# Two layers written out, a bank-by-bank end of the down projection, and the next stage's sums and splits made in quarters

## The reference, cut to what matters

```python
for l in range(DEPTH_2):                       # 2 layers
    x = x + 0.5 * swiglu(rms_norm_2(x, ffn1_norm[l]), ffn1_w_gate[l], ffn1_w_up[l], ffn1_w_down[l])
    h = rms_norm_2(x, mix_norm[l])
    z = h @ w_in[l]
    ...                                        # two attentions on z, gates g, "merged"
    x = x + merged @ w_out[l]
    x = x + 0.5 * swiglu(rms_norm_2(x, ffn2_norm[l]), ffn2_w_gate[l], ffn2_w_up[l], ffn2_w_down[l])

def rms_norm_2(x, g):
    return x * lax.rsqrt(jnp.mean(x * x, axis=-1, keepdims=True) + EPS) * g
def swiglu(x, w_gate, w_up, w_down):           # w_gate, w_up: 1024 x 2816, w_down: 2816 x 1024
    return (silu(x @ w_gate) * (x @ w_up)) @ w_down
```

## Time and profile before

| | us |
|---|---|
| runs: median (lowest to highest, 3) | 3258.0 (3250.89 to 3263.54) |
| the profiled execution, its own time | 3250.51 |
| its span | 3248.8 |
| TensorE busy | 2921.2 (90%) |
| VectorE, ScalarE, GpSimd busy | 1820.7, 1488.0, 708.0 |

### The profile page before, as it was taken

One profiled execution on the slowest core, in us unless ns is written; L12 is line 12 of the kernel. 1 busy time (PEld: TensorE's weight loads), 2 busy tenths in 40 slices (PEclk: granted clock), 3 DMA queues, 4 the chain that ended last, 5 costly groups with the idle time before them and its releaser, 6 DMA issues.

```text
span 3248.8 us, 48731 instructions
## 1 busy us (share of the span) xinstructions
PE 2921.2 (90%) x16264; PEld 2451.9 (75%) x16264; DVE 1820.7 (56%) x2469; ACT 1488.0 (46%) x2173; POOL 708.0 (22%) x353
## 2 busy tenths in 40 slices
PE   5988869996799988989999999899988979989998
PEld 3755657775599866767779988799766767779987
DVE  7544258885777334762247752877234652267743
ACT  3251337774655333653245543655234653255532
POOL 2430201110011332112421124011432113321133
PEclk8997969998899998999999999999998989999999
DMA  6610249996476231101246633566231102257623
GB/s 274 265 39 1 94 158 358 367 363 246 109 182 182 86 118 70 40 33 65 90 117 175 181 110 107 140 178 171 85 130 52 39 26 78 84 138 183 183 92 113
DMA packets 143512, 448.53 MB, mean 138 GB/s; under 512 B 13665, under 2 KB 13937, under 8 KB 141041
## 3 DMA queue, kind: packets, MB, share of 16 engines
q1 hardware_dynamic: 113136, 373.08, 32.8%
q0 software_dynamic: 28816, 63.45, 10.3%
q10 hardware_dynamic: 1456, 10.66, 0.8%
HBM read 434.55 MB, written 16.78 MB: 139 GB/s over the span
## 4 chain that ended last, share of the span: by engine, by line
PE 47%; issue 36%; POOL 7%; DVE 5%; DMA 4%; ACT 2%; POOLq 0%; SPq 0%; DVEq 0%; ACTq 0%
PE pb L1417 8%; PE pb L1418 8%; PE pb L1419 8%; POOL w_lo L483 6%; PE pb L1098 6%; PE pb L1099 6%; PE pb L1100 6%; DMA rows<-h_rows,h_idx 3%; PE pb L1105 1%; PE pb L1171 1%; DVE rs L1672 1%; DVE g_wl L2074 0%; PE pb L1226 0%; PE pb L1225 0%; PE pb L1299 0%
## 5 line engine op out<-in xcount | busy, mean ns | idle before, releaser
L483 POOL TENSOR_TENSOR w_lo<-raw,w_hi 128x1024 fp32r<-128x1024 f32 x220 | 548.0, 2492 | 1309.1 <-ACT w_hi L562 1309.1
L1417 PE MATMUL pb<-bl,g_wh 128*128 128x256 f32 x2464 | 711.8, 289 | 48.4 <-DVE bl L2124 30.0
L1418 PE MATMUL pb<-bh,g_wl 128*128 128x256 f32 x2464 | 702.0, 285 | 0.0
L1419 PE MATMUL pb<-bh,g_wh 128*128 128x256 f32 x2464 | 701.7, 285 | 0.0
L1417 PEld LDWEIGHTS pb<-bl,g_wh 128*128 128x128 f32 x2464 | 477.9, 194 | 57.4 <-DVE bl L2124 32.1
L1418 PEld LDWEIGHTS pb<-bh,g_wl 128*128 128x128 f32 x2464 | 477.9, 194 | 4.8 <-issue 4.8
L1419 PEld LDWEIGHTS pb<-bh,g_wh 128*128 128x128 f32 x2464 | 477.9, 194 | 0.0
L562 ACT ACTIVATE w_hi<-raw 128x1024 fp32r<-128x1024 f32 x220 | 231.6, 1053 | 282.1 <-PE pb L1100 267.5
L1098 PE MATMUL pb<-hl,w_hi 128*128 128x512 f32 (+1 forms) x688 | 290.0, 422 | 50.1 <-DVE hl L1683 17.3
L1098 PE MATMUL pb<-fl,w_hi 128*128 (+1 forms) x704 | 279.4, 397 | 8.8 <-DVE fl L2164 8.8
L1099 PE MATMUL pb<-bl,w_lo 128*128 128x512 f32 x704 | 279.1, 396 | 0.0
(11 more groups left out here) (366 smaller groups left out, 5360.3 us busy)
## 6 DMA issues: line engine op xcount, KB each, us to landing
raw<-in_wstream SPq DMA_DIRECT2D x220, 512.0 KB, 3.3
m_raw<-in_moe_stream SPq DMA_DIRECT2D x192, 512.0 KB, 6.3
g_own<-in_gu_stream SPq DMA_DIRECT2D x90, 512.0 KB, 5.1
raw<-in_gu_stream SPq DMA_DIRECT2D x88, 512.0 KB, 5.5
g_own<-in_gu_stream POOLq DMA_DIRECT2D x45, 512.0 KB, 5.7
raw<-in_gu_stream POOLq DMA_DIRECT2D x44, 512.0 KB, 5.8
ada_ring<-in_ada SPq DMA_DIRECT2D x8, 2048.0 KB, 7.9
g_own<-in_gu_stream SPq DMA_DIRECT2D x45, 256.0 KB, 3.5
```

Of the source, the lines that this page charges most:

```text
L483: pool.tensor_tensor(w_lo[s][:], raw[s][:], w_hi[s][:].bitcast(F32), ALU.subtract).then_inc(w_lod, 1)
L1417: pe.matmul(o, lh, rl, start=first and k == 0, stop=False, skip_group_check=True)
L1418: pe.matmul(o, ll, rh, start=False, stop=False, skip_group_check=True)
L1419: m = pe.matmul(o, lh, rh, start=False, stop=k == 3, skip_group_check=True)
```

## The change

1. The hardware loops over the layers are gone on all engines: the two layers are written one after the other, counts are constants, and the copy of a layer's vectors (line 936) is gone.
2. In each down phase the first 18 chunks stay chunk by chunk. The last four are taken bank by bank: for bank 0 all four chunks, then for bank 1, and so on. All four chunks' halves are held at once, three of them in rows of `fl` that are free by then. They still come through `raw0` and `raw1`.
3. Squares are added on GpSimd (`add_squares`: six additions into `rs`), and PE sums over partitions twice a norm (`stat_sum`), for the sum of seven squares and for the eighth.
4. x's combinations for f1, f2 and f3 are made in groups of two tiles (512 columns for each instruction) as x tiles appear: `split_early` and `low_early` for tiles 0 and 1, then 2 and 3, `split_late` and `low_late` for tiles 4 and 5, then 6 and 7. Squares are taken along with them (`take`). In the mixer this stands between the last weight chunks of w_out; `first_pair` moves there too. f0 keeps one group.
5. The first block's products stand in another order (`start`), and so do root and reciprocal for f1 to f3 (the reciprocal ahead of block 1's sums). The ACT table for the root is asked for early. After f3 no next block is prepared.
6. x is stored in four transfers of two tiles.

```diff
+TAIL = NF - 4
+FINE = ((True, slice(0, 2)), (True, slice(2, 4)), (False, slice(0, 2)), (False, slice(2, 4)))
+COARSE = ((True, slice(0, 4)), (False, slice(0, 4)))
...
+        def f_hi_of(k, s):
+            return fl[:, k - TAIL, :] if type(k) is int and k >= TAIL else fh[:, s, :]
+        def w_of(k):
+            s = k % 2
+            if k == TAIL + 2:
+                return w_hi[s][:], w_lo[s][:]
+            n = {TAIL: 0, TAIL + 1: 1, TAIL + 3: 2}[k]
+            return t_hi[n], t_lo[n]
... SP
-            sp.wait_ge(x_ready, X_L + 3 * KD * NL)
-            sp.dma_start(out, x[:]).then_inc(out_done, 16)
+            for m in range(0, KD, 2):
+                sp.wait_ge(x_ready, X_L + 3 * KD * NL - KD + m + 2)
+                sp.dma_start(out[:, m:m + 2, :], x[:, m:m + 2, :]).then_inc(out_done, 16)
... GpSimd
+            def low_tail(b0, k):
+                to_hi, to_lo = w_of(k)
+                pool.wait_ge(w_hid, 2 * b0 + k + 1)
+                pool.tensor_tensor(to_lo, raw[k % 2][:], to_hi.bitcast(F32), ALU.subtract).then_inc(w_lod, 1)
+            def add_squares(n, j):
+                pool.wait_ge(sq_ready, 3 * KD + KD * n + j + 1)
+                if j > 1:
+                    pool.wait_ge(sq_sum, (KD - 2) * n + j - 1)
+                pool.tensor_tensor(rs[:], stemp[:] if j == 1 else rs[:], root_ring[j % 2], ALU.add).then_inc(sq_sum, 1)
...
+                    for k in range(TAIL, NF):
+                        low_tail(b0, k)
+                    if h == 0:
+                        for j in range(1, KD - 1):
+                            add_squares(norm_of(f) + 1, j)
...
+                        for c in range(KD):
+                            low_one(wo + c)
+                            if c >= 3:
+                                add_squares(norm_of(f + 1), c - 2)
+                        add_squares(norm_of(f + 1), KD - 2)
... ACT
+            def split_early(f, g):
+                act.wait_ge(b_x, KD * f + 2 * g + 2 if f else 4)
+                split_11(f, g)
+                split_t1(f, g)
+            def split_late(f, g):
+                act.wait_ge(b_x, KD * f + 2 * g + 2)
+                split_21(f, g)
+                split_t2(f, g)
+                split_n3(f, g)
+                split_22(f, g)
+                split_n4(f, g)
+            def take(f, k):
+                gained(f, k)
+                square_of(norm_of(f), k, X_L - KD + 3 * KD * (f // 2) + 2 * KD * (f % 2))
+            def split_weight(b0, k):
+                act.wait_ge(w_raw[k % 2], 16 * (b0 + k // 2 + 1))
+                act.wait_ge(w_used, 2 * b0 + (TAIL - 1 if k == TAIL + 2 else 4 * (k - TAIL) + 8 if k < TAIL + 2 else 16))
+                act.activation(w_of(k)[0], raw[k % 2][:], ACT.Copy).then_inc(w_hid, 1)
...
+                for k in range(TAIL, NF):
+                    f_split(k, k % 2)
+                    split_weight(b0, k)
...
+                ffn(2 * l, 2 * NF * l, NF * l, lb)
+                act.preload_act_table(ACT.Sqrt)
+                for k in range(KD - 1):
+                    square_of(3 * l + 1, k, X_L + 3 * KD * l)
+                hi(kb, 0)
+                square_of(3 * l + 1, KD - 1, X_L + 3 * KD * l)
+                hi(kb, 1)
+                root_of_norm(3 * l + 1)
... PE
-            with pe.Fori(0, NL) as l:
-                stats(4 + 3 * l)
+            for l in range(NL):
+                stat_sum(3 * l + 1)
...
+            def stat_sum(n):
+                pe.wait_ge(sq_sum, (KD - 2) * (n + 1))
+                pe.matmul(pb[0][:], ones, rs[:], start=True, stop=False)
+                pe.wait_ge(sq_ready, 3 * KD + KD * (n + 1))
+                pe.matmul(pb[0][:], ones, root[:], start=False, stop=True).then_inc(stat_mm, 1)
...
+                    product(b, W_A11, H_N11, True, "N11")
+                    product(cc, W_S1, H_T1, True, "T1")
+                    pe.wait_ge(g_cp, 3 * Q + 1)
+                    product(b, W_S2, H_T2, False, "T2")
+                    product(a, W_A12, H_21, True, "21")
+                    pe.wait_ge(g_cp, 3 * Q + 3)
+                    product(b, W_S3, H_N3, False, "N3")
+                    if f:
+                        stat_sum(norm_of(f))
+                    product(cc, W_S4, H_N22, False, "N22")
+                    pe.wait_ge(g_c, 3 * Q + 8)
+                    product(b, W_A22, H_N4, False, "N4")
...
-                down(NF // 2 - 1, False, True)
+                for m in range(KD):
+                    for k in range(TAIL, NF):
+                        if m == 0:
+                            pe.wait_ge(w_lod, 2 * bd + k + 1)
+                            pe.wait_ge(f_lo, NF * f + k + 1)
+                        to_hi, to_lo = w_of(k)
+                        ins = mm3(pb[m][:], to_hi[:, m, :], to_lo[:, m, :], f_hi_of(k, k % 2), fl[:, k, :], False, k == NF - 1)
+                        if m == KD - 1:
+                            ins.then_inc(w_used, 1)
+                    if m < KD - 1:
+                        ins.then_inc(bank_done, 1)
... DVE
+            def low_late(f, g):
+                ks = groups(f)[g][1]
+                dve.wait_ge(b_x, KD * f + (2 * g + 2 if f else KD))
+                dve.tensor_tensor(h_t2(f, ks), bt[:, X_22, ks, :], bt[:, X_T1, ks, :], ALU.subtract).then_inc(b_t, 1)
+                dve.tensor_tensor(bt[:, X_N3, ks, :], bt[:, X_12, ks, :], bt[:, X_22, ks, :], ALU.subtract).then_inc(b_t, 1)
+                ...  # then b_low T2, 21, the sum for N4, and b_low N3, N22, N4
...
+                for g in range(KD // 2):
+                    for m in range(2 * g, 2 * g + 2):
+                        x_add(f, m)
+                    if l + 1 < NL and g < 2:
+                        low_early(f + 1, g)
+                    if l + 1 < NL and g == 2:
+                        low_late(f + 1, g)
```

More of the change, by code:

```diff
@@ L155, in build @@
         lvec_all = sb("lvec_all", [P, NL, NLVEC])
-        lvec = sb("lvec", [P, NLVEC])
         con = sb("con", [P, NCON])
@@ L827, in _, with gained @@
             hi_a22(0, 0, 0)
-            def ffn(f, Q0, n0, b0, q, gain):
-                def part(n, Q, bank, scale):
-                    act.wait_ge(g_used, 7 * Q + (8, 10, 11)[n])
+            def gained(f, k):
+                l, h = divmod(f, 2)
+                act.wait_ge(x_ready, X_L - KD + 3 * KD * l + 2 * KD * h + k + 1)
+                to = bt[:, X_11:X_12 + 1:X_12 - X_11, k, :] if k < 4 else bt[:, X_21:X_22 + 1:X_22 - X_21, k - 4, :]
+                act.activation(to, halves(x[:, k, :]), ACT.Copy, scale=LV(l, ("n1", "n2")[h], k)).then_inc(b_x, 1)
@@ new lines, in take, with ffn, part @@
+            def take(f, k):
[5 more added lines that the diff above has]
+                act.activation(w_of(k)[0], raw[k % 2][:], ACT.Copy).then_inc(w_hid, 1)
+            def ffn(f, Q0, n0, b0):
+                def part(n, Q, bank, scale, used=(8, 10, 11)):
+                    act.wait_ge(g_used, 7 * Q + used[n])
@@ L897, in ffn @@
-                hi_s31(Q0 + 1, n0, 1)
-                hi_s24(Q0 + 1)
-                for k in range(6, KD):
-                    square(q, k, root_ring)
-                Q1 = Q0 + 1
+                first, (gl, n) = (8, 10, 9), (len(groups(f)) - 1, norm_of(f))
+                if f == 0:
+                    for k in range(4):
+                        gained(f, k)
+                    split_early(f, 0)
+                    for k in range(4, KD):
+                        gained(f, k)
+                else:
+                    gained(f, KD - 1)
@@ L958, in evac @@
                     act.activation(tile, pb[bank][:], ACT.Square).then_inc(qk_sq, 1)
-                    act.activation(gained, pb[bank][:], ACT.Identity, scale=LV(gain)).then_inc(qk_gain, 1)
+                    act.activation(gained, pb[bank][:], ACT.Identity, scale=LV(l, gain)).then_inc(qk_gain, 1)
                 def root_of(n, bank, to):
@@ L1407, in _, with ffn, product @@
             stats(2, root_ring)
[L1410 to L1414 removed]
+            def stat_sum(n):
[3 more added lines that the diff above has]
+                pe.matmul(pb[0][:], ones, root[:], start=False, stop=True).then_inc(stat_mm, 1)
+            def ffn(f, Q0, b0, free):
+                def product(bank, w, b, first, name=None):
+                    if name is not None:
+                        pe.wait_ge(b_lo, PREP["lo", f, len(groups(f)) // 2 - 1 if name in ("N11", "T1") else len(groups(f)) - 1, name])
                     for k in range(4):
@@ L1463, in ffn, with down @@
                 bd = b0
-                def down(j, first, last):
+                def down(j, first):
                     for s in range(2):
```

403 lines of the change are left out of this document (248 added, 155 removed).

## The result

The changed kernel takes 3317.1 us (median of 4 runs, 3316.4 to 3327.3), the kernel before 3260.8 (4 runs, 3250.9 to 3265.8): a ratio of 1.018 with a 95% interval of 1.015 to 1.022. The forecast was 3230, range 3196 to 3252, with a chance of 0.10 on slower. It was wrong in sign.

What follows compares the result with a forecast made beforehand. TensorE was taken as the bound, busy 2921.2 of 3248.8 us, with gains only at waits and sums. Costs 36.4 and gains 60.4 gave 24 us less, forecast 3230 us; 8-in-10 range 3196 to 3252.

Steps and rivals of the forecast that it cites:

- last four chunks, waits and clock: Down-phase tails: PE waits 1.4 and 4.0 us a stage, 21.6 us in all, plus 6.8 us of lost clock.
- into the mixers: Last down matmul to the mixer's first product: 15.7 us becomes 8.8, a gain of 13.8 us for two.
- out of the mixers, to block 2: w_out's end to the third product of f1's and f3's third block: 27 us, gains of 13.3 and 12.0.
- half clock behind it: Half-clock stretches behind f1's and f3's waits at the mixer exits disappear: a gain of 5.1 us together.
- f1 into f2: From f1's end to f2's block 2: 44.2 us becomes 33, a gain of 11 us.
- w_out: Mixer's output projection: work between weight chunks makes the next chunk late, a cost of 3 us each, 6.0 in all.
- f0's start: First stage's start: PE waits some 6 us for GpSimd's sum before block 1's second product; cost 2 us with clock.
- the end: After the last matmul: one addition and a quarter's store, 9.9 us becomes 4.7, a gain of 5.2 us.
- layers written out: Both layers without a loop: cost 0, as two passes through merge and w_out code took 189.3 and 189.7 us.
- the code itself: Rival: code twice as long stalls an engine between stages, a few us each; chance 0.23 together with overfull joints.
- the rival on the slow side (+72): Waiting for chunk 21 halves the clock through the bank-by-bank tail, 19.6 us more a stage: 3302 us; chance 0.10.
- GpSimd's addition: 128 x 512 addition with two inputs, in no profile row: taken as 1.2 us, bounds 1.2 and 2.55.

Runs made afterwards that it cites:

- a_dup: Changed kernel with the gate/up stream's third quarter stored twice side by side, so its load reads 4096 bytes a partition: 3211.8 us (before 3258.6).
- b_align: Kernel before with an unused tile of 32 bytes a partition behind `lvec`, no instruction moved: 3232.4 us (before 3259.5; 0.988 to 0.994).
- b_pad300: Kernel before with 300 matmuls added to the branch that never runs: 3287.7 us (before 3256.3; 1.008 to 1.012).
- b_unroll: Kernel before with only its loop over the two layers written out on all five engines: 3341.9 us (before 3258.6; 1.021 to 1.029).
- b_shift: Kernel before, program unchanged, with 512 KB of zeros that nothing reads behind the weight stream: 3325.4 us (before 3259.5; 1.015 to 1.025).
- a_rows: Changed kernel with each gate/up block stored quarter by quarter, a quarter's rows following each other at 2048 bytes: 3214.6 us (0.983 to 0.989).
- a_far: Changed kernel with the twice-needed gate/up quarter stored twice but apart, five rows at 10240 bytes a partition, 2048-byte packets kept: 3213.4 us (before 3256.3).

## Why the prediction was wrong, point by point

Forecast and measured on the profiled runs, us:

| term | forecast | measured |
|---|---|---|
| last four chunks, waits and clock | +28.4 | +34.1 (515.5 against 481.4) |
| into the mixers | -13.8 | -13.2 |
| out of the mixers, to block 2 | -25.3 | -25.5 |
| half clock behind it | -5.1 | -4.2 (in `a_dup`) |
| f1 into f2 | -11.0 | -10.4 |
| w_out | +6.0 | +6.8 |
| f0's start | +2.0 | +4.8 |
| the end | -5.2 | -6.2 |
| layers written out | 0 | +103.9 (the stretches' 99.7, and the 4.2 above) |
| removed tile (not in the sum) | | -24 |

The last term: `b_align`'s down phases are 13.9 us shorter than before, and from a mixer's first product to w_out's end the changed kernel takes 450.1 and 449.7 us with a new wait of 3.4 in each, where before it took 451.6 twice: 10.2. In `b_align` these two stretches are 8.1 us shorter than before, so about 2 of the 24 aren't shown to be the tile's. With 1.4 us ahead of f0 all terms make the 67.3 us that the spans differ by.

- **The step that failed** is "Layers written out: 0". It was read off two passes through code that was in the loop, which can speak of fetching code and of nothing else. That a longer program may come with slower reads of an input isn't in any row of one kernel; what was there to see is that the gate/up stretch runs with its loads just in time (2.3 us of waits for them in all, and in the steady loop each waits for the one before). How little slack that left `b_pad300` shows: its loads land 0.4 to 1.5 us later than before, and its stretches take 23.4 us more. I gave no price for "a load of the steady part is later", and the rival "the code itself" got a few us between stages. Theory C, the moved instructions, has nothing left: `b_unroll` moves none and loses the same. Not tested is the change without the written-out loops; by `b_pad300` and `b_shift`, its other edits could have brought such a loss too.
- **The tail**: the mechanism was right. The changed kernel's f1, with GpSimd's two last low halves, the issue of the last chunk's transfer and its high half on ScalarE, shows both waits, 1.80 and 3.61 us where 1.4 and 4.0 were said; their sum, 5.4, is exact, here and in f2 and f3 (f0: 1.80 and 2.93).

```profile
2047.60 2.76 POOL L583 TENSOR_TENSOR w_lo<-raw,w_hi 128x1024 fp32r<-128x1024 f32 x1
2047.78 0.33 SPq L423 DMA_DIRECT2D raw<-in_wstream  x1
2050.42 0.50 PE L1292 MATMUL pb<-fl,w_hi 128*128 128x512 f32 x1 [1.80 <-POOL w_lo L583]
2051.48 1.04 ACT L1000 ACTIVATE fl<-raw 128x1024 fp32r<-128x1024 f32 x1
2052.60 2.34 POOL L583 TENSOR_TENSOR fl<-raw,fl 128x1024 fp32r<-128x1024 f32 x1 [2.24 <-ACT fl L1000]
2055.00 0.79 PE L1292 MATMUL pb<-fl 128*128 128x512 f32 x1 [3.61 <-POOL fl L583]
```

  The clock was mis-sized: 34.1 / 4 - 5.4 = 3.1 us a stage and not 1.7. It stood at half for 6.8 us of each tail in f1 to f3 (10.2 in f0) and not through the whole tail, so the rival on the slow side (+72) did not happen; the kernel was slower by another way.
- **Into the mixers** the chain is as written, to the row: root 2.6 us behind the last bank's end, then 6.49 us without a matmul.

```profile
1242.64 0.69 ACT L920 ACTIVATE root<-pb,vec 128x512 f32<-128x512 f32 x1 [0.27 <-PE pb L1608]
1243.36 3.35 DVE L1887 RECIPROCAL rs<-root 128x512 f32<-128x512 f32 x1 [2.60 <-ACT root L920]
1249.09 0.76 PE L1292 MATMUL pb<-hl,w_hi 128*128 128x512 f32 x1 [6.49 <-DVE hl L1896]
```

- **w_out**: PE waits 3.40 us for a low half, twice (3 said).

```profile
1672.87 2.53 POOL L588 TENSOR_TENSOR w_lo<-raw,w_hi 128x1024 fp32r<-128x1024 f32 x1 [6.26 <-ACT w_hi L651]
1675.53 0.49 PE L1292 MATMUL pb<-mgl,w_hi 128*128 128x512 f32 x1 [3.40 <-POOL w_lo L588]
```

- **f0's start** was under-priced, because GpSimd's addition takes 1.26 us alone and 1.62 to 2.29 beside VectorE's work, and ScalarE's squares, two in flight, wait for it:

```profile
856.00 1.62 POOL L595 TENSOR_TENSOR rs<-rs,stemp 128x512 f32<-128x512 f32 x1 [0.80 <-ACT stemp L916]
857.77 2.06 POOL L595 TENSOR_TENSOR rs<-rs,root 128x512 f32<-128x512 f32 x1
862.18 1.26 POOL L595 TENSOR_TENSOR rs<-rs,root 128x512 f32<-128x512 f32 x1
864.90 2.08 PE L1606 MATMUL pb<-rs,con 128*128 128x512 f32 x2 [7.30 <-POOL rs L595]
```

- **The end**: 0.7 us from the last matmul to the issue, and a quarter's store:

```profile
3312.36 0.69 DVE L2475 SCALAR_TENSOR_TENSOR x<-pb,x 128x512 f32<-128x512 f32 x1 [2.03 <-PE pb L1294]
3313.08 0.33 SPq L520 DMA_DIRECT2D y<-x  x1
```

- The sum of the terms that I did price comes out at -14 by measurement, -24 by forecast. The forecast total fits the kernel with its reads mended (`a_dup`, 3211.8, in the range) only with help from a term that I did not have, the removed tile. That it falls into the range is luck. The four chunks bank by bank are a loss against two: 35 us in the tails for 13 at the joints.

## What to carry to other kernels

A change that lengthens a program or an input can change the price of reads that it never touches: before its edits are blamed or praised, compare stretches that no edit touches, and the same load's landing time, in both traces. Lay a stream out so that a tile's rows don't repeat at 8192 bytes when less than the whole row is read, and start the operands of 512-column matmuls at multiples of 128 bytes. Here the first decided over up to 106 us and the second over 27, for a reordering worth 14 us by the terms above and some 37 with two chunks. When a transfer is just in time in a steady loop, price one microsecond more on it, since it is paid in every pass and again in clock.

## What the runs showed of the hardware

- **Distance between rows.** SyncE's reads of 2048 bytes at 8192 bytes from each other take 102 to 138 ns each on the mean of a run, and it changes with the length of the program or of an input; at 10240 bytes they take 105 to 111 ns in every run that has them, at 2048 bytes 97 (`a_rows` alone). The queue's 4096-byte packets don't follow it (178 to 187 ns at 8192 bytes), nor do the 2048-byte packets of GpSimd's adding transfer (199 to 208 ns in every run). The Trainium skill, "DMA: Bandwidth & Descriptors", section "Latency and other measured facts", tells of copies that slow down when a partition's rows lie a large power of two apart, 2 MiB and more, are at full rate at 512 KiB, and recover with a few KiB of padding; it calls the cause, streams that meet in the same channel of the memory, an inference. It has no figure for distances under 512 KiB; taken on downwards, 8 KiB would be harmless. The measurement decides: it came with up to 106 us more in a run, and padding mended it here too. That it is channels, no run here shows; nor how the length of a program moves an input, nor how large the loss can get.
- **Where an operand starts.** 128x512 matmuls start every 226 to 227 ns (some 231) where both operands begin at multiples of 128 bytes, every 231 to 235 where the moving one is 96 bytes past it (`hh`, `fl`, `bl` in the kernel before). For the experts' products: 233 ns with `gh` at a multiple and `m_hi` 64 bytes past, 233 with these two the other way round, 227 with both at multiples. With `hh` 64 bytes past it, 225 to 233 in one and the same run; why it varies is open. The 256-column matmuls of gate and up show none of this: 1656 of them take 198.97 us, 120 ns each, with both operands 96 bytes past a multiple (f0 before) as with both at one (f1 of `a_far`).
- **GpSimd's addition** of 128x512 takes 1.26 to 1.30 us where VectorE is idle or reads PSUM, and up to 2.29 beside VectorE's work on SBUF; 1.2 was taken. The prediction's estimate of 1.1 us, a quarter of the 2048-column figure in the Trainium skill's "GPSIMD Engine Reference", section 3.1, is 0.16 us under the undisturbed one.
